# Two-layer block on one core: split-precision products with 512 activation columns, and VectorE's weight splits ahead of a tile's burst

## The chip, the core and the metric

The kernel runs on one core of a Trainium2 chip. The metric is the device time of one execution in microseconds. Three runs of the kernel before gave 3956.96, 3957.61 and 3977.92 us, median 3957.61.

## What is computed

Two transformer-like layers over 256 positions of width 2048, in float32. Their large products are with weight matrices streamed once from HBM. The change touches the output projection and the feed-forward part of each layer:

```
# layer 1
x = x + merged @ w_out                               # 2048 x 2048
up = causal_dwconv(rmsnorm(x) @ ffn_up, ffn_conv_w)  # 2048 x 11264, 3 taps
act, val = split(up, 2)
x = x + (silu(act) * val) @ ffn_down                 # 5632 x 2048
# layer 2 (no convolution; g1, g2, sh2, sc2 from a condition)
x = x + g1 * (concat(attn, rw) @ w_out_2)
h = rmsnorm(x) * (1 + sc2) + sh2
x = x + g2 * ((silu(h @ w1) * (h @ w3)) @ w2)        # widths 5632
```

## The kernel before, in words

Activations lie transposed in SBUF, 128 channels on the partitions and T = 256 positions along the free dimension. A full-precision product is made from rounded parts. ScalarE rounds a weight tile to `w_hi` and VectorE makes the remainder `w_lo = raw - w_hi`; activations have a rounded part and a remainder too (`h_hi`, `h_lo`, `f_hi`, `f_lo`, ...). For each 128x128 block of weights TensorE adds three matmuls of 256 columns in one PSUM bank: w_lo by hi, w_hi by lo, w_hi by hi (`products`, L254 to L256). Only the first 256 of a bank's 512 columns are used for that. Part of `w_in2` (L1430) already has two activations side by side, in matmuls of 512 columns.

A weight tile is 128x1024, eight such blocks. SP's queue loads tiles in pairs (1 MB) into four chunks of `raw`. `w_hi` and `w_lo` are rings of four tiles. A round is eight tiles, k = 0 to 7, one body of a hardware loop on each engine. In `ffn_up` two tiles make one result of 128 channels: the result of tiles 0 and 1 is an act part, that of tiles 2 and 3 a val part, and so on, so a round gives four results in the banks po0 to po3. There are 22 rounds in each ffn_up, 4 in each w_out, and 12 (4 loops of 24 tiles) in each ffn_down, where a result takes six tiles, the sixth of half the width.

Each engine runs its own program in order, and semaphores join them:
- ScalarE, for each k: `split_hi(k + 3)` (L235; it waits for the landed chunk and for `used`, TensorE's count of finished tiles), then the phase's body.
- VectorE, for each k: the phase's body, then `split_lo(k + 3)` (L242; it waits for `hi_ready`). LOOK = 3 is the number of tiles that the splits are ahead of TensorE.
- TensorE waits for `lo_ready` of its tile, and at a result's first tile for the bank (`free`).
- SP's queue waits for `hi_ready` and `lo_ready` before it loads over a chunk.

The bodies in ffn_up, here called bursts: in the first layer VectorE makes the convolution of an act result, three dependent operations out of the bank, into `conv_a` (k % 4 == 1, `conv`, L2635 and L2640), and frees the bank; ScalarE waits for that and makes its Silu (L1661). At k % 4 == 3 VectorE makes the convolution of the val result into `conv_v`, multiplies it with conv_a (L1686), ScalarE rounds the product to `f_hi` (L1669) and VectorE makes `f_lo` (L1695). In the second layer there is no convolution: ScalarE makes the Silu straight from the bank (L1665) and VectorE the product straight from the bank (L1691). Behind the last f_lo of the phase TensorE begins with ffn_down. In w_out and ffn_down VectorE adds each result to x out of the bank (L2698, L2391, L1721, L1718). ScalarE loads an activation table once at a round's first rounding and once at its first Silu.

Of the kernel before, what the change touches and what calls it, by code (L numbers as in the profile page):

```python
# [14 lines left out]
F32R = mybir.dt.float32r  # L15
# [6 lines left out]
P = 128  # L22
# [71 lines left out]
def program(nc, d):  # L94

    ctx = ExitStack()
    with ctx:
# [30 lines left out]
        h_hi, h_lo, hc_hi, hc_lo = hh[:, 0, 0], hh[:, 0, 1], hh[:, 1, 0], hh[:, 1, 1]  # L128
        hf = sb("hf", [KD, T], TMP)
# [62 lines left out]
        m_hi = sb("m_hi", [KD, T], A0 + 32, F32R)  # L192
        m_lo = sb("m_lo", [KD, T], A0 + 48, F32R)
        f_hi = sb("f_hi", [KF, T], A0, F32R)
        f_lo = sb("f_lo", [KF, T], A0 + 44, F32R)
# [63 lines left out]
        def project(pe, phase, rounds, act_hi, act_lo, k_tiles, r_off=0, t_off=0, split=None):  # L259
# [3 lines left out]
            with pe.Fori(0, rounds) as i:  # L263
                rnd = i + (ROUND0[phase] + r_off)
                for k in range(8):
# [3 lines left out]
                    if split is not None and k < 2:  # L269
                        pe.wait_ge(*sv.at(split, ("lo1", "lo3")[k]))  # L270
                    if half == 0:
                        turn = i * (per // 4) + (TURN0[phase] + t_off + o // 4)
                    products(pe, rnd, k, [(s, half * 8 + s) for s in range(8)], o % 4, act_hi, act_lo,
                             half == 0, half == 1 or k_tiles == 8, turn).then_inc(used, 1)

        def project_down(pe, phase):

            with pe.Fori(0, 4) as i:
                for q in range(24):
                    rnd, k, o, s = i * 3 + (ROUND0[phase] + q // 8), q % 8, q // 6, q % 6  # L280
                    tiles = [(t, s * 8 + t) for t in range(8 if s < 5 else 4)]
                    products(pe, rnd, k, tiles, o, f_hi, f_lo, s == 0, s == 5,
                             i + TURN0[phase] if s == 0 else None).then_inc(used, 1)
# [112 lines left out]
        conv_sum = sem("conv_sum")  # L396
# [960 lines left out]
        o_hi = sb("o_hi", [KD, T], H0, F32R)  # L1357
        o_lo = sb("o_lo", [KD, T], H0 + 16, F32R)
# [350 lines left out]
        def ffn_down_dve(dve, phase, f, final=False):  # L1709
            def body(i, final):  # L1710
                for q in range(24):
                    rnd = i * 3 + (ROUND0[phase] + q // 8)
                    if q % 6 == 5:
# [3 lines left out]
                        if f:  # L1717
                            dve.scalar_tensor_tensor(xt, po[o][:, 0:T], mod[:, ds(i * 4 + (80 + o), 1)], xt,  # L1718
                                                     ALU.mult, ALU.add).then_inc(free[o], 1)
                        else:  # L1720
# [1208 lines left out]
```

## Time and profile before

| | us |
|---|---|
| median of three runs | 3957.61 |
| the profiled execution | 3957.27 |
| its span, first to last instruction | 3955.6 |
| TensorE busy with matmuls | 3623.4 |
| VectorE busy | 2283.2 |
| ScalarE busy | 1655.2 |
| first ffn_up, TensorE's first to last matmul | 1067 to 1576 |
| first ffn_down | 1580 to 1836 |
| second ffn_up | 3165 to 3673 |
| second ffn_down | 3675 to 3931 |
| w_out of the layers | 953 to 1046, 3047 to 3142 |

Engines: PE is TensorE's matmul, PEld its weight load, DVE VectorE, ACT ScalarE. A row in order of time begins with its start and duration in us, and ends with the time for which the engine had been idle before it and what it waited for. A matmul's duration in such rows is longer than the distance between two of them, since they are pipelined; what counts is how often one starts. The granted clock of TensorE is 1.00 at 2.4 GHz and 0.50 at 1.2 GHz.

### The profile page before, as it was taken

How to read it: one execution, taken by the hardware profiler on the slowest of the kernel's cores; microseconds unless marked ns; L12 is line 12 of the kernel's file. 1: busy time of each engine (PE TensorE's matmuls, PEld its weight loads, DVE VectorE, ACT ScalarE, POOL GpSimd, SP SyncE). 2: the span in 40 equal slices, each digit the busy share in tenths (PEclk: the TensorE clock that was granted, in tenths of full speed). 3: DMA queues.
4: the chain of work that ended last, by engine and by line, in shares of the span. 5: the costliest groups of instructions: out<-in, count | busy, mean ns of one | idle time of the engine just before them, and what ended most of it. 6: DMA issues, size and time to landing. Idle time of an engine off the chain costs nothing.

```text
span 3955.6 us, 83548 instructions
## 1 busy us (share of the span) xinstructions
PE 3623.4 (92%) x33580; PEld 3302.6 (83%) x33580; DVE 2283.2 (58%) x4062; ACT 1655.2 (42%) x2387; POOL 24.2 (1%) x47
## 2 busy tenths in 40 slices
PE   7999998998899999997899977778788899999998
PEld 5998886878899999997688844666666899999998
DVE  4659995665577777444443533666665444444443
ACT  4545563223355554333212333443442355555333
POOL 0000000000000000000000000000000000000000
PEclk9999998999999999998899997888887999999999
DMA  4546664444355555553223363000001445555553
GB/s 156 180 145 262 257 254 165 160 171 143 134 185 176 190 180 178 176 183 133 73 96 117 139 213 117 5 7 6 7 5 57 148 170 181 182 188 178 174 181 115
DMA packets 80722, 572.11 MB, mean 145 GB/s; under 512 B 9488, under 2 KB 9744, under 8 KB 15472
## 3 DMA queue, kind: packets, MB, share of 16 engines
q1 hardware_dynamic: 78048, 558.50, 40.3%
q0 software_dynamic: 2448, 10.46, 0.8%
q8 instruction: 159, 2.61, 0.3%
q14 instruction: 67, 0.55, 0.0%
HBM read 566.82 MB, written 2.10 MB: 144 GB/s over the span
## 4 chain that ended last, share of the span: by engine, by line
PE 77%; DVE 15%; issue 3%; ACT 2%; DMA 2%; DVEq 0%; ACTq 0%; SPq 0%; POOL 0%
PE po L254 17%; PE po L255 17%; PE po L256 17%; PE po L1430 6%; DVE w_lo L242 2%; PE pa L300 2%; PE pa L989 2%; PE po L989 1%; PE po L418 1%; DMA raw<-ada 1%; DVE s_v L680 1%; PE pa L897 1%; PE po L468 1%; DVE hf L311 1%; PE po L469 1%
## 5 line engine op out<-in xcount | busy, mean ns | idle before, releaser
L242 DVE TENSOR_TENSOR w_lo<-raw,w_hi 128x1024 fp32r<-128x1024 f32 x880 | 1039.8, 1200 | 459.3 <-ACT w_hi L235 444.2
L235 ACT ACTIVATE w_hi<-raw 128x1024 fp32r<-128x1024 f32 (+1 forms) x877 | 897.8, 1037 | 803.1 <-PE po L256 582.1
L254 PE MATMUL po<-hh,w_lo 128*128 128x256 f32 x3744 | 1064.9, 284 | 24.4 <-DVE hh L335 12.6
L255 PE MATMUL po<-hh,w_hi 128*128 128x256 f32 x3744 | 1060.9, 283 | 0.0
L256 PE MATMUL po<-hh,w_hi 128*128 128x256 f32 x3744 | 1060.9, 283 | 0.0
L254 PEld LDWEIGHTS po<-hh,w_lo 128*128 128x128 f32 x3744 | 720.3, 192 | 30.4 <-issue 29.8
L255 PEld LDWEIGHTS po<-hh,w_hi 128*128 128x128 f32 x3744 | 720.3, 192 | 0.3
L256 PEld LDWEIGHTS po<-hh,w_hi 128*128 128x128 f32 x3744 | 720.1, 192 | 0.0
L254 PE MATMUL po<-f_hi,w_lo 128*128 128x256 f32 x1408 | 400.0, 284 | 6.1 <-DVE f_lo L1695 6.1
L255 PE MATMUL po<-f_lo,w_hi 128*128 128x256 f32 x1408 | 399.9, 284 | 0.0
L256 PE MATMUL po<-f_hi,w_hi 128*128 128x256 f32 x1408 | 399.8, 284 | 0.0
L254 PEld LDWEIGHTS po<-f_hi,w_lo 128*128 128x128 f32 x1408 | 271.7, 193 | 6.5 <-issue 6.5
L256 PEld LDWEIGHTS po<-f_hi,w_hi 128*128 128x128 f32 x1408 | 271.9, 193 | 0.0
L255 PEld LDWEIGHTS po<-f_lo,w_hi 128*128 128x128 f32 x1408 | 271.8, 193 | 0.0
L1430 PE MATMUL po<-hh,w_hi 128*128 128x512 f32 x704 | 218.1, 391 | 0.0
L1430 PEld LDWEIGHTS po<-hh,w_hi 128*128 128x128 f32 x704 | 133.0, 189 | 27.8
L468 PE MATMUL po<-hh,w_lo 128*128 128x256 f32 x512 | 154.3, 301 | 0.0
L1669 ACT ACTIVATE f_hi<-conv_v 128x256 f32 x88 | 36.7, 418 | 278.5 <-DVE conv_v L1686 166.1
L1430 PE MATMUL po<-hh,w_lo 128*128 128x512 f32 x352 | 137.8, 391 | 15.9 <-DVE hh L335 15.9
L470 PE MATMUL po<-hh,w_hi 128*128 128x256 f32 x512 | 145.7, 284 | 0.0
L469 PE MATMUL po<-hh,w_hi 128*128 128x256 f32 x512 | 145.5, 284 | 0.0
L300 PE MATMUL pa<-hf,ones 128*128 128x256 f32 x224 | 60.4, 437 | 53.1 <-ACT hf L291 53.1
(543 smaller groups left out, 6337.8 us busy)
## 6 DMA issues: line engine op xcount, KB each, us to landing
raw<-ffn_up SPq DMA_DIRECT2D x176, 1024.0 KB, 4.8
raw<-w_in SPq DMA_DIRECT2D x112, 1024.0 KB, 4.9
raw<-ada SPq DMA_DIRECT2D x96, 1024.0 KB, 6.3
raw<-ffn_down SPq DMA_DIRECT2D x64, 1024.0 KB, 4.9
raw<-w_out SPq DMA_DIRECT2D x32, 1024.0 KB, 4.8
raw<-ffn_down SPq DMA_DIRECT2D x32, 768.0 KB, 4.2
raw<-glu SPq DMA_DIRECT2D x16, 1024.0 KB, 6.4
raw<-dn_proj SPq DMA_DIRECT2D x8, 1024.0 KB, 5.1
```

Of the source, the lines that this page charges most:

```text
L235: act.activation(w_hi[:, k % 4, 0:width], raw[:, k // 2 % ring, (k % 2) * PW:(k % 2) * PW + width], ACT.Copy).then_inc(hi_ready, 1)
L242: dve.tensor_tensor(w_lo[:, k % 4, 0:width], raw[:, k // 2 % ring, (k % 2) * PW:(k % 2) * PW + width], w_hi[:, k % 4, 0:width].bitcast(F32 ...
L254: pe.matmul(po[bank][:, 0:T], lo, act_hi[:, t, :], start=first and n == 0, stop=False)
L255: pe.matmul(po[bank][:, 0:T], hi, act_lo[:, t, :], start=False, stop=False)
L256: mm = pe.matmul(po[bank][:, 0:T], hi, act_hi[:, t, :], start=False, stop=end)
L300: mm = pe.matmul(pa[0][:, 0:T], ones[:], hf[:, t, :], start=t == 0, stop=t == KD - 1)
L311: last = dve.scalar_tensor_tensor(out[:, t, :], x[:, t, :], w(t), rstd[:], ALU.mult, ALU.mult)
L468: pe.matmul(bank(i * per + o), lo, act_hi[:, t, :], start=first, stop=False)
L469: pe.matmul(bank(i * per + o), hi, act_lo[:, t, :], start=False, stop=False)
L470: mm = pe.matmul(bank(i * per + o), hi, act_hi[:, t, :], start=False, stop=end)
L989: mm[e] = pe.matmul(o, lhs[e][r, m, :], w, start=True, stop=True)
L1430: mm = pe.matmul(po[o % 4][:].rearrange("p (s t) -> p s t", s=2), w, hh[:, ::-1, part, t, :], start=half == 0 and n == 0 and w is lo, stop ...
```

## The change

1. `products_wide` takes the place of `products` in w_out, ffn_up and ffn_down of both layers. The rounded activations and their remainders lie side by side (`h_both`, `m_both`, `f_both`, `o_both`). For a 128x128 block there are two matmuls: w_hi by both parts, 512 columns into the whole bank, and w_lo by the rounded part, 256 columns into its first half.
2. The two halves of a bank must be added. In w_out and ffn_down `add_to_x` adds first the one and then the other to x. In ffn_up ScalarE copies the upper half to conv_a or conv_v (`upper`), VectorE adds it to the lower half in the bank (`summed`), and only then comes what came before: convolution, Silu, product.
3. `round_dve` issues `split_lo(k + LOOK)` ahead of the body in both ffn_up phases, and behind it, as before, in all others. ScalarE's order of `split_hi` and body is not changed.

The other products of the kernel (w_in, glu, dn_proj, w_in2) stay as they are. The diff, cut to its core:

```diff
+        m_both = sb("m_both", [2, KD, T], A0 + 32, F32R)
+        m_hi, m_lo = m_both[:, 0], m_both[:, 1]
+        f_both = sb("f_both", [2, KF, T], A0, F32R)
+        f_hi, f_lo = f_both[:, 0], f_both[:, 1]
...
+        def products_wide(pe, rnd, k, tiles, bank, both, first, last, turn=None):
+            if turn is not None:
+                pe.wait_ge(free[bank], turn)
+            pe.wait_ge(lo_ready, rnd * 8 + k + 1)
+            for n, (s, t) in enumerate(tiles):
+                hi = w_hi[:, k % 4, s * P:s * P + P]
+                lo = w_lo[:, k % 4, s * P:s * P + P]
+                end = last and n == len(tiles) - 1
+                pe.matmul(po[bank][:].rearrange("p (s t) -> p s t", s=2), hi, both[:, :, t, :],
+                          start=first and n == 0, stop=False)
+                mm = pe.matmul(po[bank][:, 0:T], lo, both[:, 0, t, :], start=False, stop=end)
+            return mm
...
+        def project_wide(pe, phase, rounds, both, split=None):
+            with pe.Fori(0, rounds) as i:
+                rnd = i + ROUND0[phase]
+                for k in range(8):
+                    o, half = k // 2, k % 2
+                    if split is not None and k < 2:
+                        pe.wait_ge(*sv.at(split, ("lo1", "lo3")[k]))
+                    products_wide(pe, rnd, k, [(s, half * 8 + s) for s in range(8)], o, both, half == 0, half == 1,
+                                  i + TURN0[phase] if half == 0 else None).then_inc(used, 1)
...
+        def add_to_x(dve, n, bank, xt, scale=None):
+            for h, part in enumerate(halves):
+                if h:
+                    dve.wait_ge(summed, n + 1)
+                if scale is None:
+                    last = dve.tensor_tensor(xt, po[bank][:, part], xt, ALU.add)
+                else:
+                    last = dve.scalar_tensor_tensor(xt, po[bank][:, part], scale, xt, ALU.mult, ALU.add)
+                if h == 0:
+                    last.then_inc(summed, 1)
+            return last
...
         def ffn_up_act(act, phase, f, round_act):
             def body(i, rnd, k):
                 j = i * 2 + k // 4
+                if k % 2:
+                    act.wait_ge(used, rnd * 8 + k + 1)
+                    if k % 4 == 1:
+                        act.wait_ge(ff_prod, j + KF * f)
+                    settle(act)
+                    upper_half = conv_v if k % 4 == 3 else conv_a
+                    act.activation(upper_half[:], po[k // 2][:, T:2 * T], ACT.Copy).then_inc(upper, 1)
                 if k % 4 == 1 and f == 0:
                     act.wait_ge(*freed(phase, i, 4, k // 2))
                     act.activation(conv_a[:], conv_a[:], ACT.Silu).then_inc(ff_silu, 1)
                 if k % 4 == 1 and f == 1:
-                    act.wait_ge(used, rnd * 8 + k + 1)
-                    act.wait_ge(ff_prod, j + KF)
+                    act.wait_ge(summed, i * 4 + (SUM0[phase] + k // 2 + 1))
                     act.activation(conv_a[:], po[k // 2][:, 0:T], ACT.Silu).then_inc(free[k // 2], 1)
...
                 at = i * 8 + (CONV0 + 2 * o)
+                if k % 2:
+                    n = i * 4 + (SUM0[phase] + o)
+                    dve.wait_ge(upper, i * 4 + (88 * f + o + 1))
+                    upper_half = conv_v if k % 4 == 3 else conv_a
+                    dve.tensor_tensor(po[o][:, 0:T], po[o][:, 0:T], upper_half[:], ALU.add).then_inc(summed, 1)
+                    dve.wait_ge(summed, n + 1)
                 if k % 4 == 1 and f == 0:
-                    dve.wait_ge(used, rnd * 8 + k + 1)
                     conv(dve, conv_a[:], o, w, 3, at).then_inc(free[o], 1)
                 if k % 4 == 3:
-                    dve.wait_ge(used, rnd * 8 + k + 1)
                     if f == 0:
                         conv(dve, conv_v[:], o, w, 3, at).then_inc(free[o], 1)
...
             def round_dve(dve, phase, rounds, body, r_off=0):
                 with dve.Fori(0, rounds) as i:
                     for k in range(8):
+                        if phase in ("ffn_up", "ffn_up2"):
+                            split_lo(dve, i + (ROUND0[phase] + r_off), k + LOOK)
                         body(i, i + (ROUND0[phase] + r_off), k)
-                        split_lo(dve, i + (ROUND0[phase] + r_off), k + LOOK)
+                        if phase not in ("ffn_up", "ffn_up2"):
+                            split_lo(dve, i + (ROUND0[phase] + r_off), k + LOOK)
```

`project_wide` and `project_down` call `products_wide`; the waits for SUM0 count the results of all phases.

## Rows read from the trace of the kernel before

**Rows 1.** The page: busy time, chain by line, DMA issues of ffn_up

```profile
PE 3623.4 (92%) x33580; PEld 3302.6 (83%) x33580; DVE 2283.2 (58%) x4062; ACT 1655.2 (42%) x2387; POOL 24.2 (1%) x47
...
PE po L254 17%; PE po L255 17%; PE po L256 17%; PE po L1430 6%; DVE w_lo L242 2%; PE pa L300 2%; PE pa L989 2%; PE po L989 1%; PE po L418 1%; DMA raw<-ada 1%; DVE s_v L680 1%; PE pa L897 1%; PE po L468 1%; DVE hf L311 1%; PE po L469 1%
...
raw<-ffn_up SPq DMA_DIRECT2D x176, 1024.0 KB, 4.8
```

**Rows 2.** Windows of three stages: busy us (instructions) of engines, granted clock

```profile
1067.00:1576.50 509.50, 509.29 (x4224) 509.09 (x4224) 367.32 (x524) 261.25 (x307) 0.00 (x0) 0.99 0.52 179
1580.50:1835.70 255.20, 255.16 (x2112) 254.99 (x2112) 112.20 (x111) 93.92 (x96) 0.00 (x0) 0.99 0.53 179
3165.00:3673.40 508.40, 508.35 (x4224) 508.18 (x4224) 244.54 (x269) 266.55 (x306) 0.00 (x0) 1.00 0.53 180
```

**Rows 3.** Windows: narrow products (ffn_up), wide products (w_in2)

```profile
1100.00:1550.00 450.00, 450.00 (x3752) 450.00 (x3752) 327.81 (x471) 232.18 (x274) 0.00 (x0) 1.00 0.53 182
...
1950.00:2100.00 150.00, 150.00 (x663) 124.21 (x662) 61.13 (x67) 29.16 (x28) 0.00 (x0) 1.00 0.28 97
```

**Rows 4.** ScalarE in order of time, second ffn_up: a Silu

```profile
3404.11 0.38 ACT L1665 ACTIVATE conv_a<-po 128x256 f32<-128x256 f32 x1
```

**Rows 5.** VectorE in order of time, first ffn_up: start, us, operation

```profile
1075.54 0.48 DVE L2635 TENSOR_SCALAR conv_a<-po,par 128x256 f32<-128x256 f32 x1 [5.17 <-PE po L256]
...
1190.27 1.22 DVE L242 TENSOR_TENSOR w_lo<-raw,w_hi 128x1024 fp32r<-128x1024 f32 x1 [0.62 <-ACT w_hi L235]
...
1199.64 0.42 DVE L1695 TENSOR_TENSOR f_lo<-conv_v,f_hi 128x256 f32 x1 [0.85 <-ACT f_hi L1669]
1199.98 2.35 DVE L242 TENSOR_TENSOR w_lo<-raw,w_hi 128x1024 fp32r<-128x1024 f32 x2
1202.35 0.48 DVE L2635 TENSOR_SCALAR conv_a<-po,par 128x256 f32<-128x256 f32 x1
1202.97 1.11 DVE L2640 SCALAR_TENSOR_TENSOR conv_a<-po,par,conv_a 128x255 f32<-128x255 f32 x2
1204.00 1.21 DVE L242 TENSOR_TENSOR w_lo<-raw,w_hi 128x1024 fp32r<-128x1024 f32 x1
1205.52 1.22 DVE L242 TENSOR_TENSOR w_lo<-raw,w_hi 128x1024 fp32r<-128x1024 f32 x1 [0.31 <-ACT w_hi L235]
1208.00 0.48 DVE L2635 TENSOR_SCALAR conv_v<-po,par 128x256 f32<-128x256 f32 x1 [1.26 <-PE po L256]
...
1209.87 0.43 DVE L1686 TENSOR_TENSOR conv_v<-conv_v,conv_a 128x256 f32<-128x256 f32 x1
1211.13 0.42 DVE L1695 TENSOR_TENSOR f_lo<-conv_v,f_hi 128x256 f32 x1 [0.84 <-ACT f_hi L1669]
```

**Rows 6.** Groups of w_in2 by shape: busy us, mean ns | idle before

```profile
L1458 DVE TENSOR_SCALAR zkv<-po,ts 128x512 f32 x13 | 9.8, 750 | 78.5 <-PE po L1430 78.5
```

**Rows 7.** ScalarE in order of time, first ffn_up

```profile
1199.32 1.99 ACT L235 ACTIVATE w_hi<-raw 128x1024 fp32r<-128x1024 f32 x2
1204.12 0.42 ACT L1661 ACTIVATE conv_a<-conv_a 128x256 f32<-128x256 f32 x1 [2.81 <-DVE conv_a L2640]
1204.44 1.99 ACT L235 ACTIVATE w_hi<-raw 128x1024 fp32r<-128x1024 f32 x2
...
1210.92 1.28 ACT L235 ACT_TABLE_LOAD   x1
1212.22 2.01 ACT L235 ACTIVATE w_hi<-raw 128x1024 fp32r<-128x1024 f32 x2
```

**Rows 8.** End of the first ffn_up: VectorE's last f_lo, TensorE's next matmul

```profile
1579.76 0.43 DVE L1695 TENSOR_TENSOR f_lo<-conv_v,f_hi 128x256 f32 x1 [0.84 <-ACT f_hi L1669]
...
1580.54 0.43 PE L254 MATMUL po<-f_hi,w_lo 128*128 128x256 f32 x1 [4.05 <-DVE f_lo L1695]
```

**Rows 9.** Windows of 2 us behind that gap: TensorE busy, granted clock

```profile
1582.00:1584.00 2.00, 2.00 (x12) 0.50 0.26 39
1584.00:1586.00 2.00, 2.00 (x18) 0.97 0.84 326
```

More of the change, by code:

```diff
@@ L128, in program @@
         h_hi, h_lo, hc_hi, hc_lo = hh[:, 0, 0], hh[:, 0, 1], hh[:, 1, 0], hh[:, 1, 1]
+        h_both = hh[:, 0]
         hf = sb("hf", [KD, T], TMP)
@@ L191, in program @@
         yd_lo = sb("yd_lo", [8, T], H0 + 24, F32R)
[L192 to L195, printed above, removed]
+        m_both = sb("m_both", [2, KD, T], A0 + 32, F32R)
+        m_hi, m_lo = m_both[:, 0], m_both[:, 1]
+        f_both = sb("f_both", [2, KF, T], A0, F32R)
+        f_hi, f_lo = f_both[:, 0], f_both[:, 1]
         po = [ctx.enter_context(nc.psum_tensor(f"po{n}", [P, 512], F32)) for n in range(4)]
@@ L257, in products, with project @@
             return mm
-        def project(pe, phase, rounds, act_hi, act_lo, k_tiles, r_off=0, t_off=0, split=None):
+        def products_wide(pe, rnd, k, tiles, bank, both, first, last, turn=None):
[10 more added lines that the diff above has]
+            return mm
+        def project(pe, phase, rounds, act_hi, act_lo, k_tiles, r_off=0, t_off=0):
             per = 8 if k_tiles == 8 else 4
@@ L268, in project @@
                     turn = None
-                    if split is not None and k < 2:
-                        pe.wait_ge(*sv.at(split, ("lo1", "lo3")[k]))
                     if half == 0:
@@ L281, in project_down @@
                     tiles = [(t, s * 8 + t) for t in range(8 if s < 5 else 4)]
-                    products(pe, rnd, k, tiles, o, f_hi, f_lo, s == 0, s == 5,
-                             i + TURN0[phase] if s == 0 else None).then_inc(used, 1)
+                    products_wide(pe, rnd, k, tiles, o, f_both, s == 0, s == 5,
+                                  i + TURN0[phase] if s == 0 else None).then_inc(used, 1)
+        SUM0 = {"w_out": 0, "ffn_up": 16, "ffn_down": 104, "w_out2": 120, "ffn_up2": 136, "ffn_down2": 224}
+        halves = [slice(0, T), slice(T, 2 * T)]
+        def add_to_x(dve, n, bank, xt, scale=None):
[9 more added lines that the diff above has]
+            return last
         def down_width(q):
@@ L395, in program @@
         branch_lo, ones_set = sem("branch_lo"), sem("ones_set")
-        conv_sum = sem("conv_sum")
+        conv_sum, summed, upper = sem("conv_sum"), sem("summed"), sem("upper")
         CONV0 = 72
@@ L1356, in program @@
         k_S, k_ur = pair("k_S", [P], 84.5, 0.5), pair("k_ur", [P], 85.5, 0.5)
-        o_hi = sb("o_hi", [KD, T], H0, F32R)
-        o_lo = sb("o_lo", [KD, T], H0 + 16, F32R)
+        o_both = sb("o_both", [2, KD, T], H0, F32R)
+        o_hi, o_lo = o_both[:, 0], o_both[:, 1]
         def order(e):
@@ L1716, in body @@
                         dve.wait_ge(used, rnd * 8 + q % 8 + 1)
[L1717 to L1720, printed above, removed]
-                            dve.tensor_tensor(xt, po[o][:, 0:T], xt, ALU.add).then_inc(free[o], 1)
+                        add_to_x(dve, i * 4 + (SUM0[phase] + o), o, xt,
+                                 mod[:, ds(i * 4 + (80 + o), 1)] if f else None).then_inc(free[o], 1)
                     if not final or q + LOOK < 24:
@@ L2390, in on_out @@
                     dve.wait_ge(used, rnd * 8 + k + 1)
-                    dve.scalar_tensor_tensor(xt, po[o][:, 0:T], mod[:, ds(i * 4 + (32 + o), 1)], xt,
-                                             ALU.mult, ALU.add).then_inc(free[o], 1)
+                    add_to_x(dve, i * 4 + (SUM0["w_out2"] + o), o, xt, mod[:, ds(i * 4 + (32 + o), 1)]).then_inc(free[o], 1)
             round_dve(dve, "w_out2", 4, on_out)
@@ L2425, in block2_pe @@
             rk_pe(pe)
-            project(pe, "w_out2", 4, o_hi, o_lo, 16, split=4)
+            project_wide(pe, "w_out2", 4, o_both, 4)
             norm_pe(pe, 5)
-            project(pe, "ffn_up2", 22, h_hi, h_lo, 16, split=5)
+            project_wide(pe, "ffn_up2", 22, h_both, 5)
             pe.wait_ge(ff_lo, 2 * KF)
@@ L2697, in on_out @@
                     dve.wait_ge(used, rnd * 8 + k + 1)
-                    dve.tensor_tensor(xt, po[o][:, 0:T], xt, ALU.add).then_inc(free[o], 1)
+                    add_to_x(dve, i * 4 + (SUM0["w_out"] + o), o, xt).then_inc(free[o], 1)
             round_dve(dve, "w_out", 4, on_out)
@@ L2747, in _ @@
             pe.wait_ge(mrg_lo, 16)
-            project(pe, "w_out", 4, m_hi, m_lo, 16)
+            project_wide(pe, "w_out", 4, m_both)
             norm_pe(pe, 1)
-            project(pe, "ffn_up", 22, h_hi, h_lo, 16, split=1)
+            project_wide(pe, "ffn_up", 22, h_both, 1)
             pe.wait_ge(ff_lo, KF)
```

## The prediction

> **What bounds the kernel now.** I read the page first, then the windows by stage, then TensorE's pitch, then VectorE and ScalarE in order of time within one round. The page has TensorE busy for 92% of the span and 51% of the chain of work that ended last in the three matmuls of `products`, 17% in each [rows 1]. The change touches six stages (w_out, ffn_up and ffn_down of both blocks). The windows of three of them have TensorE busy throughout, at a granted clock of 0.99 to 1.00 [rows 2]; the second ffn_down and the two w_out are like the ffn_down shown. In all six the time is the number of matmuls by their pitch. The same rows give VectorE's load: 367.3 of 509.5 us in the first ffn_up, 244.5 of 508.4 in the second, 112 of 255 in ffn_down. So there is one place where VectorE has little to spare, and it is there that I look for the next bound.
>
> **What the wider product brings.** A 256-column matmul starts every 450/3752 = 119.9 ns, a 512-column one every 150/663 = 226.2 ns, both at granted clock 1.00 [rows 3]. A weight tile costs three of the first kind today, 359.8 ns, and will cost one of each, 346.2 ns. That saves 13.7 ns a tile. No stage before has the two widths in turn, so the bounds are 0 and 13.7 ns; I take the upper one, since the wide rows already load new weights for each matmul. Tiles: 22 rounds of 64 in each ffn_up (1408, a third of the 4224 matmuls of [rows 2]), 704 in each ffn_down, 256 in each w_out. TensorE's own time then falls by 19.3 us in each ffn_up, 9.6 in each ffn_down, 3.5 in each w_out: 64.8 us in all. A round of ffn_up goes from 23.03 to 22.15 us on TensorE.
>
> The Trainium skill (TensorE: Matmul & The Clock Gate, Back-to-back issue gap) puts a warm gap at the columns over 2.4 GHz plus about 2.5 ns. By that the saving would be 2.5 ns a tile and 12 us in all. The two rows disagree with it: each has about 13 ns over its columns. The measurement decides.
>
> **What it adds.** Each result now lies in two halves of a bank. In ffn_up ScalarE copies the upper half to SBUF and VectorE adds it to the lower half in the bank, 88 times a phase, before anything else is done with it. The copy is priced by the Silu that reads the same 128x256 out of a bank, 0.38 us [rows 4]. For the add there is no VectorE arithmetic with its output in a bank. The nearest is the 128x256 product of two tensors, 0.43 us; a dependent operation starts 0.14 us behind an end (conv_a at 1202.35, 0.48 long, the next at 1202.97) [rows 5]. I take the two together, 0.57 us a step. Bounds: 0.34 us, the start-to-start of an f_lo and the w_lo behind it (1199.64 to 1199.98) [rows 5], and 0.90 us, that of the arithmetic out of a bank at 512 columns, 0.75, with the same gap [rows 6].
> In w_out and ffn_down `add_to_x` makes one operation into two, the second 0.57 us behind the first. VectorE is idle there for over half the time [rows 2], so it costs only at the phase's end: 0.6 us, four times. At the end of the second ffn_up copy and add stand before the product: 0.38 + 0.04 + 0.57 and a little for the wait, 1.1 us.
>
> **The moved split, the step that decides.** In both ffn_up phases VectorE now does `split_lo` of tile k+3 ahead of the burst of tile k. ScalarE's program keeps its order: `split_hi`, then its body, whose Silu waits for conv_a and whose f_hi waits for the product. So the split that follows a burst is now the one whose w_hi is queued behind that burst on ScalarE. Today another split lies between, with its w_hi ready long before.
> - After conv_a: today conv_a ends at 1204.08, the Silu starts at 1204.12, the next w_hi at 1204.44, and the w_lo that needs it at 1205.52 [rows 5, 7]. That is 1.44 us, of which the w_lo at 1204.00 covers all but 0.31. Moved, it stands ahead of the burst and covers nothing: VectorE waits 1.44 us, twice a round.
> - After f_lo: w_hi comes behind f_hi at 1199.32; it takes 1.04 us and 0.04 to VectorE (1204.44 to 1205.52), so its w_lo can start at 1200.40, 0.76 us after f_lo's start at 1199.64. Once a round a table load stands between: w_hi at 1212.22 gives 1213.30, 2.17 us after f_lo's 1211.13 [rows 5, 7]. Today a w_lo lies in this gap too, and the wait that is left is the 0.62 us at 1190.27 [rows 5].
>
> VectorE's chain through half a round, from the steps of [rows 5, 7]: four w_lo at 1.16, between 2.35 - 1.21 and half of 1199.98 to 1202.35 (4.64), two adds (1.14), conv_a to its end at 1204.08 (1.74 with rounding), the wait behind it (1.44), conv_v to the product (1.87), product to f_lo (1.26), f_lo to the next w_lo (0.76). That is 12.85 us; the half with the table load has 1.41 more, 14.26. A round is 27.1 us, against 22.15 on TensorE and 23.03 today. In the first ffn_up TensorE is no longer the bound. Of it 5.1 us are waits for w_hi (1.44 twice, and 0.76 and 2.17 less 0.34 each for the f_lo). Without them a round would be 22.0 us, so the adds alone use up nearly all that VectorE had spare.
>
> The Trainium skill (ScalarE: Activation LUTs, What ACT_TABLE_LOAD costs) states about 2.66 us for a switch of tables, with a drain behind the load. By it a round would be 1.4 us longer. The trace has w_hi 0.02 us behind a load of 1.28 us (1210.92 to 1212.22) [rows 7], so no drain is paid here.
>
> **The phase.** Its first conv_a starts today at 1075.54, cold clock included [rows 5]; copy and first add put the chain's start at 1076.0. From there to the last f_lo's end are 22 x 27.11 less two w_lo (2.3) and the last wait (1.7): 592.4 us, so 1668.4. Today f_lo ends at 1580.2 [rows 8]. That is +88.2 us. TensorE then sits idle for some 8 us in place of 4.05, and restarts at the lower clock for a little longer than the 3.5 us that 4.05 us of idling cost it (back to 0.97 by 1584) [rows 8, 9]: +1, an estimate.
>
> In the second ffn_up there is no conv. VectorE's chain there is 19.9 us a round (27.1 less two conv_a of 1.74 and two conv_v of 1.87), so TensorE stays the bound. The look-ahead holds too: from the end of tile 3 to w_lo of tile 7 are copy with its hand-overs 0.57, add 0.57, product 0.43 + 0.19, f_hi 0.33, table load 1.28, w_hi 1.08, w_lo 1.21 = 5.7 us, and TensorE has three tiles, 8.3 us. Weight DMAs wait in SP's queue for w_lo of a chunk freed four chunks earlier; later splits delay the issue, but their 4.8 us to landing [rows 1] fit in the five tiles, over 13 us, that remain.
>
> **The sum** against the profiled execution, 3957.27 us (span 3955.6 and 1.7 around it; the median of the runs, 3957.61, is 0.3 above it): first ffn_up +88.2 + 1.0; second -19.3 + 1.1; two ffn_down -19.2 + 1.2; two w_out -7.0 + 1.2. Together +47.2, which gives 4004 us.
>
> **The rivals.**
> - *TensorE stays the bound everywhere*, because ScalarE runs further ahead of VectorE than I have it, and look-ahead hides the waits: -64.8 and some 4.6 for longer ends give 3897. It decides if VectorE's round stays under 22.15. For it speaks only that VectorE has 28% idle time now; against it that Silu and f_hi cannot start before VectorE's burst and are ahead of the w_hi in the same queue. Chance 0.07.
> - *Half hidden*: the waits behind conv_a shrink to the 0.31 of today and the one with the table load to 0.62 [rows 5]. A round is 27.1 - 2.3 - 1.2 = 23.6 us, the first ffn_up costs 22 x 0.57 = +13 less 1 for its start, the other stages keep -41: 3928. With a round of 25.0 us the whole comes out even. Chance 0.08 for all up to 3977.
> - *The clock falls in the gaps.* TensorE will idle 5 us a round, most at once at the table load: the two w_lo before it and the one behind it span 1.16 + 7.04 us, less two tiles of 2.77, 2.7 us. After 4.05 us idle the granted clock was at its lower level for some 3.5 us [rows 8, 9]. If each round's long gap did that, TensorE would lose about 2 us of its 5 us of slack: no price. Only if it held for most of a round would TensorE be the bound, at about 33 us: 4130. Chance 0.05.
> - *The wide product saves nothing beside a narrow one*: the 45.5 us of gain in the other five stages is gone, 4050. Chance 0.05.
> - *Forecast*, VectorE's chain sets the first ffn_up at 26.4 to 28.6 us a round: 0.75.
>
> **Range.** The add's bounds move 88 steps by -0.23 and +0.33 us: -20 and +29. The new waits, each an instruction on VectorE with no row for itself, and clock losses can add to 10. 3980 to 4045 holds a little under 0.8. 0.5% of 3957 is about what a measurement of this kernel can tell from no change: faster 0.10, same 0.06, slower 0.84.
>
> **What will show it.** Right: the first ffn_up takes about 601 us to its last f_lo in place of 513, VectorE is busy for about 80% of it and its longest idle groups are w_lo waiting for ScalarE's w_hi, about 1.44 and 2.1 us each; TensorE shows gaps ahead of the matmul after a w_lo; the second ffn_up shows none and takes 489 us. Wrong: w_lo waits of 0.3 to 0.6 us in the first ffn_up with TensorE busy throughout (the rivals of hidden waits); matmul pitches that add up to 360 ns a tile (the wide product); a granted clock well under 0.9 in the first ffn_up (the clock); an add of 128x256 far from 0.43 us (its price).

## The result and the profile after

The changed kernel took 4021.25 us, the median of six runs (4001.59 to 4037.9), beside 3963.3 us for the kernel before (six runs, 3955.48 to 3984.26). The ratio on record is 1.0124, with a 95% interval of 1.0095 to 1.0152: slower by 1.2%. (The two medians divided give 1.0146, inside that interval.) Its profiled execution is the shortest of the six, 4001.59 us with a span of 3999.9, and 44.3 us of span over the one before.

The page of the changed kernel (busy time; shares of the chain that ended last, by engine and by line) answers to [rows 1]:

```profile
PE 3607.7 (90%) x28844; PEld 3062.8 (77%) x28844; DVE 2387.4 (60%) x4302; ACT 1707.8 (43%) x2563; POOL 24.2 (1%) x47
...
PE 62%; DVE 20%; issue 10%; ACT 5%; DMA 2%; DVEq 1%; ACTq 0%; SPq 0%; POOL 0%
PE po L270 19%; PE po L272 10%; PE po L1475 6%; PE po L255 3%; PE po L256 3%; PE po L257 3%; DVE w_lo L243 3%; ACT w_hi L236 2%; PE pa L345 1%; PE pa L1034 1%; PE po L1034 1%; PE po L463 1%; DMA raw<-ada 1%; DVE conv_v L2694 1%; DVE conv_a L2694 1%
```

TensorE has 28844 matmuls in place of 33580, and yet its share of the chain is down (it was 77% before), with VectorE at 20% (15%), ScalarE at 5% (2%) and issue at 10% (3%). Windows over the first ffn_up, the first ffn_down and the second ffn_up of the changed kernel (busy us and instructions of PE, PEld, DVE, ACT, POOL; granted clock; DMA) answer to [rows 2]:

```profile
1064.20:1655.60 591.40, 533.50 (x2816) 448.47 (x2816) 399.68 (x610) 281.94 (x390) 0.00 (x0) 0.96 0.44 153
1664.10:1910.50 246.40, 246.38 (x1408) 216.95 (x1408) 117.83 (x125) 93.95 (x95) 0.00 (x0) 0.99 0.55 185
3235.60:3725.40 489.80, 489.79 (x2816) 431.72 (x2816) 284.94 (x357) 295.20 (x393) 0.00 (x0) 1.00 0.53 186
```

The last two are as full of matmuls as before and shorter, 246.4 for 255.2 and 489.8 for 508.4 us. The first has a third fewer matmuls than in [rows 2], takes 591.4 us in place of 509.5, and leaves TensorE idle for 58 of them.

Span by stage in us, from TensorE's first matmul in one to its first in the next (the middle begins with the first `pa<-hf,ones` behind the first ffn_down):

| stage | before | after | difference | forecast |
|---|---|---|---|---|
| up to the first w_out | 952.6 | 950.0 | -2.6 | 0 |
| first w_out and norm | 114.6 | 114.1 | -0.5 | -2.9 |
| first ffn_up | 513.3 | 599.9 | +86.6 | +88.2 |
| first ffn_down and norm | 274.6 | 266.3 | -8.3 | -9.0 + 1.0 |
| middle, without a part of the change | 1191.9 | 1192.4 | +0.4 | 0 |
| second w_out and norm | 118.0 | 112.9 | -5.1 | -2.9 |
| second ffn_up | 510.5 | 493.0 | -17.5 | -18.2 |
| second ffn_down, norm, end | 280.1 | 271.4 | -8.7 | -9.0 |

One round of the first ffn_up, VectorE in order of time in the changed kernel (start, us, operation, idle before it); the rows answer to [rows 5]:

```profile
1180.83 0.43 DVE L1732 TENSOR_TENSOR po<-po,conv_a 128x256 f32<-128x256 f32 x1
...
1193.70 0.43 DVE L1732 TENSOR_TENSOR po<-po,conv_a 128x256 f32<-128x256 f32 x1
1194.27 0.48 DVE L2689 TENSOR_SCALAR conv_a<-po,par 128x256 f32<-128x256 f32 x1
1194.90 1.11 DVE L2694 SCALAR_TENSOR_TENSOR conv_a<-po,par,conv_a 128x255 f32<-128x255 f32 x2
1197.44 2.36 DVE L243 TENSOR_TENSOR w_lo<-raw,w_hi 128x1024 fp32r<-128x1024 f32 x2 [1.43 <-ACT w_hi L236]
1199.72 0.43 DVE L1732 TENSOR_TENSOR po<-po,conv_v 128x256 f32<-128x256 f32 x1
1200.30 0.48 DVE L2689 TENSOR_SCALAR conv_v<-po,par 128x256 f32<-128x256 f32 x1
...
1202.16 0.43 DVE L1741 TENSOR_TENSOR conv_v<-conv_v,conv_a 128x256 f32<-128x256 f32 x1
1203.45 0.42 DVE L1750 TENSOR_TENSOR f_both<-conv_v,f_both 128x256 f32 x1 [0.86 <-ACT f_both L1720]
1205.60 2.36 DVE L243 TENSOR_TENSOR w_lo<-raw,w_hi 128x1024 fp32r<-128x1024 f32 x2 [1.72 <-ACT w_hi L236]
1207.87 0.43 DVE L1732 TENSOR_TENSOR po<-po,conv_a 128x256 f32<-128x256 f32 x1
```

The two w_lo at 1197.44 and at 1205.60 stand directly behind a burst, each with an idle time for w_hi: 1.43 and 1.72 us. The add into the first bank of a half-round starts at 1180.83, 1193.70 and 1207.87: 12.87 and 14.17 us, a round of 27.04. Between their starts the rounds of this phase take 27.04 to 27.06 us, all but the first, 27.37. ScalarE in the same stretch, which answers to [rows 7]:

```profile
1196.05 0.42 ACT L1713 ACTIVATE conv_a<-conv_a 128x256 f32<-128x256 f32 x1 [3.44 <-DVE conv_a L2694]
1196.37 1.99 ACT L236 ACTIVATE w_hi<-raw 128x1024 fp32r<-128x1024 f32 x2
...
1202.78 0.42 ACT L1720 ACTIVATE f_both<-conv_v 128x256 f32 x1 [4.15 <-DVE conv_v L1741]
1203.21 1.28 ACT L236 ACT_TABLE_LOAD   x1
1204.51 2.00 ACT L236 ACTIVATE w_hi<-raw 128x1024 fp32r<-128x1024 f32 x2
```

It does the Silu at 1196.05 as conv_a ends, and only then the w_hi at 1196.37 that VectorE is waiting for; and f_hi at 1202.78, the table load, then w_hi at 1204.51. The waits of the changed kernel in that phase, 1100 to 1600 us (total, times, longest):

```profile
DVE w_lo L243 <- ACT w_hi L236: 89.9, 74, 1.7
PEld po L270 <- DVE w_lo L243: 67.5, 56, 2.7
PE po L270 <- DVE w_lo L243: 48.1, 31, 2.3
```

Here w_lo waited 89.9 us for w_hi; of that 81.5 lie in 1100 to 1550 us, the stretch in which the kernel before had 23.5. That TensorE waits for w_lo is new: the narrow kernel shows no such wait in this phase. The end of the phase, TensorE's next matmul with its idle time, against 4.05 us of idling in [rows 8]:

```profile
1664.07 0.79 PE L270 MATMUL po<-f_both,w_hi 128*128 128x512 f32 x1 [8.46 <-DVE f_both L1750]
```

### The profile page after: what moved, and what is told of

It is laid out like the page before. It is cut to its first block, busy times and chain, and to the rows that moved or that the text cites. A ratio compares the mean times of both kernels' runs of the same rounds, so it can differ in the third digit from the quotient of the medians.

```text
span 3999.9 us, 75190 instructions
## 1 busy us (share of the span) xinstructions
PE 3607.7 (90%) x28844; PEld 3062.8 (77%) x28844; DVE 2387.4 (60%) x4302; ACT 1707.8 (43%) x2563; POOL 24.2 (1%) x47
## 4 chain that ended last, share of the span: by engine, by line
PE 62%; DVE 20%; issue 10%; ACT 5%; DMA 2%; DVEq 1%; ACTq 0%; SPq 0%; POOL 0%
PE po L270 19%; PE po L272 10%; PE po L1475 6%; PE po L255 3%; PE po L256 3%; PE po L257 3%; DVE w_lo L243 3%; ACT w_hi L236 2%; PE pa L345 1%; PE pa L1034 1%; PE po L1034 1%; PE po L463 1%; DMA raw<-ada 1%; DVE conv_v L2694 1%; DVE conv_a L2694 1%
## 5 line engine op out<-in xcount | busy, mean ns | idle before, releaser
L270 PE MATMUL po<-hh,w_hi 128*128 128x512 f32 x2816 | 1015.2, 403 | 82.2 <-DVE w_lo L243 55.9
L270 PEld LDWEIGHTS po<-hh,w_hi 128*128 128x128 f32 x2816 | 539.7, 192 | 225.5 <-DVE w_lo L243 78.0
L270 PE MATMUL po<-f_both,w_hi 128*128 128x512 f32 x1408 | 490.4, 394 | 11.6 <-DVE f_both L1750 11.6
L272 PE MATMUL po<-f_both,w_lo 128*128 128x256 f32 x1408 | 393.2, 279 | 0.0
L270 PEld LDWEIGHTS po<-f_both,w_hi 128*128 128x128 f32 x1408 | 264.8, 188 | 72.0 <-issue 12.2
L272 PEld LDWEIGHTS po<-f_both,w_lo 128*128 128x128 f32 x1408 | 266.5, 189 | 0.0
L256 PE MATMUL po<-hh,w_hi 128*128 128x256 f32 x928 | 262.7, 283 | 0.0
L257 PE MATMUL po<-hh,w_hi 128*128 128x256 f32 x928 | 262.7, 283 | 0.0
L1475 PE MATMUL po<-hh,w_hi 128*128 128x512 f32 x704 | 217.8, 391 | 0.0
L256 PEld LDWEIGHTS po<-hh,w_hi 128*128 128x128 f32 x928 | 178.1, 192 | 0.3
L257 PEld LDWEIGHTS po<-hh,w_hi 128*128 128x128 f32 x928 | 178.1, 192 | 0.0
L1475 PEld LDWEIGHTS po<-hh,w_hi 128*128 128x128 f32 x704 | 133.1, 189 | 27.6
L515 PE MATMUL po<-hh,w_hi 128*128 128x256 f32 x512 | 145.8, 285 | 0.0
L514 PE MATMUL po<-hh,w_hi 128*128 128x256 f32 x512 | 145.5, 284 | 0.0
```

The costliest lines, as they stand in the source:

```text
L256: pe.matmul(po[bank][:, 0:T], hi, act_lo[:, t, :], start=False, stop=False)
L257: mm = pe.matmul(po[bank][:, 0:T], hi, act_hi[:, t, :], start=False, stop=end)
L270: pe.matmul(po[bank][:].rearrange("p (s t) -> p s t", s=2), hi, both[:, :, t, :], start=first and n == 0, stop=False)
L272: mm = pe.matmul(po[bank][:, 0:T], lo, both[:, 0, t, :], start=False, stop=end)
L514: pe.matmul(bank(i * per + o), hi, act_lo[:, t, :], start=False, stop=False)
L515: mm = pe.matmul(bank(i * per + o), hi, act_hi[:, t, :], start=False, stop=end)
```

## The experiments

Theory: the w_lo behind a burst waits for a w_hi which ScalarE's queue holds behind the same burst; with the adds in the burst, VectorE's chain is longer than TensorE's round. Rivals: the copies and adds alone are more than VectorE can do; or the clock, which falls in TensorE's gaps, sets the time of a round. Phase lengths below are of the first ffn_up, first matmul to ffn_down's first, 513.3 us before and 599.9 after.

**1. The split back behind the burst**, in the changed kernel:

```diff
-                        if phase in ("ffn_up", "ffn_up2"):
-                            split_lo(dve, i + (ROUND0[phase] + r_off), k + LOOK)
                         body(i, i + (ROUND0[phase] + r_off), k)
-                        if phase not in ("ffn_up", "ffn_up2"):
-                            split_lo(dve, i + (ROUND0[phase] + r_off), k + LOOK)
+                        split_lo(dve, i + (ROUND0[phase] + r_off), k + LOOK)
```

> The changed kernel with one part undone: VectorE's burst comes ahead of split_lo again in both ffn_up phases; wide products, copies and adds stay. Theory (the split behind a burst waits for a w_hi that is queued behind that burst on ScalarE): the waits of w_lo for w_hi in the first ffn_up fall from 1.43 and 1.72 us to 0.3 to 0.6, a round takes 23.4 us in place of 27.0, the phase loses about 79 us, and the whole is 3922 us against 4001.6 of the changed kernel's profiled execution, under the 3957 of before. Rival (the copies and adds are what VectorE cannot carry, whatever the order): a round stays within 1 us of 27.0 and the whole at about 4000. Rival (the clock falls in TensorE's gaps and sets the pace): the gaps stay, since the adds stay, and the whole is over 3970.

The phase took 531.0 us, 68.9 less than in the changed kernel. The whole was 3955.35 us at a ratio of 0.9972 (0.9954 to 0.9989) to the kernel before. Two adds of VectorE one round apart, and the total wait of w_lo (1100 to 1550 us):

```profile
1305.55 0.43 DVE L1732 TENSOR_TENSOR po<-po,conv_a 128x256 f32<-128x256 f32 x1
...
1329.44 0.43 DVE L1732 TENSOR_TENSOR po<-po,conv_a 128x256 f32<-128x256 f32 x1
...
DVE w_lo L243 <- ACT w_hi L236: 22.7, 57, 0.6
```

The rounds here take 23.9 us, 0.5 over the forecast, and the wait of w_lo for w_hi is 22.7 us for the changed kernel's 81.5, with the copies and adds still there. The rival of the adds expected 27 us and is out; that of the clock expected a whole over 3970. Yet with the better order the wide phase is still 17.7 us longer than the narrow one. In the second ffn_up the order makes no difference: 493.0 us here and in the changed kernel. The profiled execution, 3961.5 us, is 39 over the forecast: 10 in this phase, 17 in the middle, where the change has no part and this execution took 1209.6 us, 7 ahead of the first w_out and 5 in the last ffn_down. Number 8 deals with the middle and with ffn_down. The 7 us stay unexplained: that first stretch, the same in all kernels, took 950.0 to 957.8 us over the profiles.

**2. The order alone**, in the kernel before, which keeps its narrow products and has no adds:

```diff
                     for k in range(8):
+                        if phase in ("ffn_up", "ffn_up2"):
+                            split_lo(dve, i + (ROUND0[phase] + r_off), k + LOOK)
                         body(i, i + (ROUND0[phase] + r_off), k)
-                        split_lo(dve, i + (ROUND0[phase] + r_off), k + LOOK)
+                        if phase not in ("ffn_up", "ffn_up2"):
+                            split_lo(dve, i + (ROUND0[phase] + r_off), k + LOOK)
```

> The kernel before with one part added: split_lo ahead of the burst in both ffn_up phases; products stay at 256 columns, no copies, no adds. Theory: without the adds VectorE's chain through a round is 27.1 less 4 x 0.57, that is 24.8 us, over TensorE's 23.03, so the first ffn_up takes about 36 us longer and the whole is 3993 us; the second ffn_up is unchanged. Rival (the order alone is free, and only wide products with it cost time): 3957 us, rounds of 23.03.

3995.16 us, ratio 1.0083 (1.0050 to 1.0115); the phase took 547.9 us, 34.6 more than before. Two f_lo of VectorE one round apart, 24.65 us, and the wait of w_lo, now four times the 23.5 us of before:

```profile
1312.49 0.42 DVE L1695 TENSOR_TENSOR f_lo<-conv_v,f_hi 128x256 f32 x1 [0.85 <-ACT f_hi L1669]
...
1337.14 0.42 DVE L1695 TENSOR_TENSOR f_lo<-conv_v,f_hi 128x256 f32 x1 [0.85 <-ACT f_hi L1669]
...
DVE w_lo L242 <- ACT w_hi L235: 90.7, 73, 1.8
```

The order costs 35 us without the adds and 69 with them (number 1): half of its price is there with the narrow burst already. The other half is most simply read as slack that the adds have used up, since the narrow round had been set by TensorE; no run shows it by itself.

**3. ScalarE's w_hi ahead of its part of the burst**, in the changed kernel:

```diff
                     act.activation(upper_half[:], po[k // 2][:, T:2 * T], ACT.Copy).then_inc(upper, 1)
+                    if k < 7 or not last_round:
+                        split_hi(act, rnd, k + 1 + LOOK)
...
-            round_act(act, phase, 22, body)
+            split_hi(act, ROUND0[phase], LOOK)
+            def ahead(i, last_round=False):
+                for k in range(8):
+                    if k % 2:
+                        split_hi(act, i + ROUND0[phase], k + LOOK)
+                    body(i, i + ROUND0[phase], k, last_round)
+            with act.Fori(0, 21) as i:
+                ahead(i)
+            ahead(21, True)
```

> The changed kernel, with ScalarE's order changed as well: in ffn_up it issues the w_hi of tile k+4 right behind the copy of tile k's upper half and ahead of the Silu or f_hi, so the w_lo behind a burst finds its w_hi ready. Theory: the waits of 1.43 us go, a round is VectorE's busy time and inner waits, 22.0 to 23.1 us against TensorE's 22.15; the first ffn_up takes about 85 us less than in the changed kernel, the whole is 3916 us. Rival (VectorE is loaded beyond its share whoever makes w_hi ready): over 3960.

3941.86 us, ratio 0.9939 (0.9916 to 0.9961). The phase took 519.1 us, 81 less than in the changed kernel, with VectorE's order as the change has it. Two adds one round apart (23.33 us) and the wait of w_lo:

```profile
1418.97 0.43 DVE L1742 TENSOR_TENSOR po<-po,conv_a 128x256 f32<-128x256 f32 x1
...
1442.30 0.43 DVE L1742 TENSOR_TENSOR po<-po,conv_a 128x256 f32<-128x256 f32 x1
...
DVE w_lo L243 <- ACT w_hi L236: 21.2, 58, 0.5
```

VectorE does the same work in the same order, and 81 of the 87 us are gone, because another engine's queue was changed. That is the theory's main test. The round of 23.33 us is a little over the 22.0 to 23.1 expected; w_lo still waits 21.2 us for w_hi in 450 us, about 1.1 us a round. The expectation had the wait gone. The whole is 26 us over its forecast: 4 in this phase, 10 in the second ffn_up (503.5 us, a slower pace of matmuls), 8 ahead of the first w_out and 2 in the second.

**4. Half of the table loads**, in the changed kernel:

```diff
-            round_act(act, phase, 22, body)
+            with act.Fori(0, 11) as i2:
+                for h in range(2):
+                    i = i2 * 2 + h
+                    for k in range(8):
+                        split_hi(act, i + ROUND0[phase], k + LOOK)
+                        body(i, i + ROUND0[phase], k)
```

> The changed kernel with ScalarE's ffn_up loops over two rounds in one body, so that the two table loads come once in two rounds; nothing else. Theory: every second wait of 1.72 us at the first w_lo behind an f_lo falls to 0.31; rounds alternate between 27.0 and 25.7 us, the first ffn_up takes 14 us less, the whole is 3987 us. Rival (the load is hidden behind something else that is late): 4000 to 4003.

The phase took 584.4 us, 15.5 less for 11 loads fewer ahead of a w_hi, 1.4 us each: the 1.28 us of the load stood wholly on the chain. The rounds alternate between 27.05 and 25.64 us, as forecast. The whole, 4007.52 us at 1.0119 (1.0084 to 1.0154), doesn't tell this apart from the changed kernel. In the profile half of the saving was lost again ahead of the first w_out (957.8 us for 950.0) and 3.9 us in the first ffn_down, at a slower pace of matmuls.

**5. The narrow kernel with the early split and ScalarE ahead**, number 2 with ScalarE's loop as in number 3:

```diff
             def body(i, rnd, k, last_round=False):
                 j = i * 2 + k // 4
+                if k % 2:
+                    act.wait_ge(used, rnd * 8 + k + 1)
+                    if k < 7 or not last_round:
+                        split_hi(act, rnd, k + 1 + LOOK)
...
```

> The narrow kernel with split_lo first, as in the run before of that kind (548 us in the first ffn_up, 3995 us), and ScalarE's w_hi of tile k+4 ahead of its Silu and f_hi. Theory (the order costs time only since w_hi is queued behind the burst): the waits of w_lo for w_hi go, TensorE is the bound again with rounds of 23.03 us, the first ffn_up takes 513 us and the whole is that of the kernel before, 3957 us, within 5. Rival (VectorE's early split costs time by itself): over 3975.

3964.93 us, ratio 1.0001 (0.9982 to 1.0021), phase 513.8 us for the 513.3 of before. Number 2's 34.6 us are gone but for 0.5. The profiled execution took 3979.7 us; 19 us of that lie in the middle. ScalarE now waits for TensorE, w_lo waits for w_hi less than half as long as in number 2 (34.9 us for 90.7), and TensorE waits for neither (1100 to 1550 us):

```profile
ACT w_hi L235 <- PE po L256: 125.4, 97, 1.9
...
DVE w_lo L242 <- ACT w_hi L235: 34.9, 59, 1.0
```

**6. A third of the matmul time left out.** In the first ffn_up the matmul with w_lo is not made, so the remainder of the weights is missing from its results:

```diff
-                pe.matmul(po[bank][:].rearrange("p (s t) -> p s t", s=2), hi, both[:, :, t, :],
-                          start=first and n == 0, stop=False)
+                mm = pe.matmul(po[bank][:].rearrange("p (s t) -> p s t", s=2), hi, both[:, :, t, :],
+                               start=first and n == 0, stop=skip and end)
+                if skip:
+                    continue
...
```

> The changed kernel with a part of the computation left out: in the first ffn_up TensorE makes only the matmul of 512 columns for each block, the one with w_lo is not made, so TensorE's work in a round falls from 22.15 to 14.5 us at full clock. Everything of VectorE and ScalarE stays. Theory (VectorE's chain with its waits for ScalarE sets the phase): rounds of 27.0 us, the first ffn_up takes 600 us as before, at most 6 us more if the clock stays at its lower level, where 64 matmuls of 512 columns take 27.3 us. Rival (TensorE, by its gaps and its clock, has a share in the 27.0 us): the phase falls by over 20 us.

This kernel ran once, in 4027.97 us. The phase took 597.6 us against 599.9. Matmuls were half as many, TensorE was busy for 352.6 of 500 us, the granted clock fell to 0.84 (0.96 in the changed kernel), and TensorE's longest wait in a round grew from 2.3 to 4.2 us. The window, and the matmuls behind one such gap (those behind the next start at 1211.09, a round of 27.03 us):

```profile
1100.00:1600.00 500.00, 352.59 (x1184) 264.81 (x1184) 338.17 (x517) 240.87 (x335) 0.00 (x0) 0.84 0.44 155
...
1184.06 10.37 PE L270 MATMUL po<-hh,w_hi 128*128 128x512 f32 x32 [4.21 <-DVE w_lo L243]
```

With a third less to do on TensorE, and a lower clock, the round is the same: neither has a share in the 27.0 us. That ends the rival of the clock.

**7. The whole change out of the first ffn_up only**; the other five stages stay wide:

```diff
-            project_wide(pe, "ffn_up", 22, h_both, 1)
+            project(pe, "ffn_up", 22, h_hi, h_lo, 16, split=1)
...
-                if k % 2:
+                if k % 2 and f == 1:
                     act.wait_ge(used, rnd * 8 + k + 1)
...
-                        if phase in ("ffn_up", "ffn_up2"):
+                        if phase == "ffn_up2":
...
```

> The changed kernel with the whole change taken out of the first ffn_up alone (three matmuls of 256 columns, no copies, no adds, burst first); the other five stages stay wide. Theory: the first ffn_up is back at 513 us, the others keep what they gained in the changed kernel's profile (8.3 + 17.5 + 8.7 + 0.5 + 5.1 = 40 us), so the whole is 3917 us where matmul pairs start every 346 ns, and up to 22 us more (3328 pairs of 6.6 ns) where they start every 353 ns, as they did in single stages of the last two profiles. Rival (the wide product saves nothing that lasts): 3957.

3933.63 us, ratio 0.9915 (0.9892 to 0.9938). The phase is at 513.2 us. This version beats both kernels, by 0.85% and about 2%. It is near the upper end of the 3917 to 3939 us expected. In its profile (3938.97 us) both ffn_down stages ran at the slower pace that number 8 looks into, 10 us together, and the middle was 10 us longer than in the changed kernel's.

**8. What the two paces come from.** A pair is the two matmuls of one 128x128 block, 512 columns and 256. In the profiles of numbers 3 and 4 some wide stages took 353 ns for a pair in place of 346; so did the first w_out of the changed kernel's own profile. Two kernels put a tile's eight matmuls of 512 columns ahead of its eight of 256, one on number 7 and one on the changed kernel; a third is the changed kernel again:

```diff
                 pe.matmul(po[bank][:].rearrange("p (s t) -> p s t", s=2), hi, both[:, :, t, :],
                           start=first and n == 0, stop=False)
+            for n, (s, t) in enumerate(tiles):
+                lo = w_lo[:, k % 4, s * P:s * P + P]
+                end = last and n == len(tiles) - 1
                 mm = pe.matmul(po[bank][:, 0:T], lo, both[:, 0, t, :], start=False, stop=end)
```

> The kernel of the run before it in this set, with a weight tile's eight matmuls of 512 columns first and its eight of 256 behind them, in place of one of each in turn. Theory of the two paces (346 or 353 ns a pair comes from the widths in turn; wide ones in a row took 226.2 and narrow ones 119.9 in all profiles): every stage shows 346 ns, the whole is 3917 us with a narrower spread. Rival (the pace belongs to the execution or the stage, not to the order): some stages show 353 ns again and the spread is that of the run before.

> The changed kernel with its products grouped in the same way, eight of 512 columns and then eight of 256; nothing else. Theory: in the first ffn_up VectorE's chain sets the time, rounds of 27.0 us as in the changed kernel whatever TensorE's order; in the other stages 346 ns a pair in every one; the whole is 4000 us with a spread of under 15 us. Rival (TensorE's pace matters in the first ffn_up too): its rounds differ from 27.0.

> The changed kernel once more, unchanged, for a second profile beside the first, whose 3999.9 us of span was the shortest of six. Theory: rounds of 27.0 us in the first ffn_up again; what is longer lies in the other stages, as pairs of matmuls at 353 ns in place of 346 (up to 22 us in all), and in the recurrences of the second layer (its middle, which took 1192 to 1210 us in the profiles so far, with no part of the change in it). Rival (the first ffn_up varies, by the clock in TensorE's gaps): its rounds differ from 27.0 by over 0.3 us.

The second ffn_up in windows of 350 us (busy us and matmuls of PE first), the changed kernel's first profile:

```profile
3250.00:3600.00 350.00, 350.00 (x2021) 308.74 (x2021) 202.78 (x252) 213.92 (x285) 0.00 (x0) 1.00 0.54 188
```

The changed kernel again, its first ffn_up and its second:

```profile
1065.70:1657.30 591.60, 533.80 (x2816) 448.89 (x2816) 399.64 (x610) 282.13 (x390) 0.00 (x0) 0.96 0.44 153
3300.00:3650.00 350.00, 350.00 (x1984) 303.36 (x1983) 198.47 (x248) 210.96 (x280) 0.00 (x0) 1.00 0.53 185
```

Grouped, on number 7:

```profile
3200.00:3550.00 350.00, 350.00 (x2009) 308.11 (x2008) 201.10 (x250) 211.88 (x282) 0.00 (x0) 1.00 0.53 187
```

These are 2 x 350 / 2021 = 346.4 ns a pair, 352.8, and 348.4; taken from start to start, 346.6, 353.3 and 349.1. Nothing differs between the first two programs. In a stage in which TensorE does not stop, the pace held from its first microseconds to its last, and it changed from stage to stage. Grouping gave a time in between (349.1 ns from start to start in every wide stage of both grouped kernels but the first ffn_up, where TensorE waits), not the 346 that the theory of the order wanted, so that theory fell. The wholes were 3934.09 us at 0.9921 (0.9891 to 0.9951), 4015.81 us at 1.0143 (1.0111 to 1.0175) and 4027.04 us at 1.0145 (1.0116 to 1.0174): no gain from grouping that can be told. What sets the pace stays open, but the traces show when it is set. In number 3's first ffn_up TensorE stops for a moment about every 12 us, and each run of matmuls between two stops has one of the two paces: 30 pairs from 1138.34 to 1148.74 us, 346.8 ns each, and 30 from 1161.66 to 1172.26, 353.3 ns each. A stop can change the pace, and between stops it stays.

The first ffn_up took 599.8 us grouped and 600.2 us in the repetition, against 599.9: it does not vary. The 35 us between the two profiles of the changed kernel lie in the middle (1209.5 us for 1192.4, 17), in the second ffn_up (502.3 for 493.0, 9) and in the ffn_down behind it (278.7 for 271.4, 7), both at 353 ns. The middle contains the second layer's recurrence, where TensorE has short matmuls with gaps between. From its first matmul `pa<-k_S,k_ah` to its last (TensorE's busy time, granted clock), in the changed kernel and in its repetition:

```profile
2559.10:3104.30 545.20, 439.61 (x9086) 0.85 0.02 6
...
2556.50:3123.10 566.60, 464.39 (x9087) 0.79 0.02 6
```

The same matmuls take 25 us more of TensorE's time at the lower clock, and the stretch is 21 us longer; the rest of the middle is 4 us shorter. Over all twelve profiles the stretch's length goes with the clock, from 540.6 us at 0.87 (the kernel before) to 565.3 at 0.78 (number 1). This speaks for the clock as the source of the difference, though no run sets it, and why it is lower there in one execution than in another isn't shown.

## Why the prediction was right

Forecast 4004 us, measured 4001.6 in the profile with 4021 as the median, on the side and within the range.

- **The bound moves to VectorE in the first ffn_up.** Right, to the term. Chain: 27.11 us a round forecast, 27.04 measured. Waits behind conv_a: 1.44 forecast, 1.43. With the table load, from f_lo's start to w_lo's: 2.17 forecast, 2.15 measured (1203.45 to 1205.60). Add: 0.57 a step forecast, 0.57 from 1193.70 to 1194.27; its 0.43 us with the output in a bank are those of the product with the output in SBUF. Numbers 3, 5 and 6 show that it is ScalarE's queue and not TensorE or the order by itself.
- **The phase.** +88.2 forecast, +86.6 measured. TensorE's gap at its end was 8.46 us for the 8 forecast.
- **The other five stages.** -42.0 us forecast, and +1.0 for the restart that falls into the first ffn_down; -40.1 measured. That this sum fits so well is in part luck. The two w_out, forecast at -2.9 each, came at -0.5 and -5.1: the first ran at the slower pace, and of the second's gain up to 2.3 us may be none, since that stage took 115.7 us in the narrow kernel of number 5 and 118.0 in that of before. The second ffn_up has no wait of TensorE for w_lo, as the look-ahead of 5.7 against 8.3 us said.
- **The wide product.** The forecast's 13.7 ns is for a 128x128 block, which it calls a tile; from start to start it is 360.0 less 346.6, 13.4 ns. That held in all but one of the five stages of this profile that are bound by TensorE, and it is the best case: at 353 ns a pair the saving is 7 ns. Over the 3328 blocks of these stages the slower pace costs up to 21 us. It was not among the rivals.
- **The median.** The 17 us between forecast and median were not foreseen, and that the profiled execution, the shortest of six, came within 3 us of the forecast is luck to that extent. The forecast started from 3957 us, and the kernel before has a median of 3963.3 over six runs: 6 of the 17 us. The first profile, like the forecast, has the good pace nearly everywhere and a short middle. The repetition has 17 us more in the middle and 16 in two stages at the slow pace. The middle took 1185 to 1211 us over the eleven profiles of the changed kernel and the experiments, 1191.9 in that of before; its length goes with the granted clock in the recurrence (number 8), in narrow and wide kernels alike.
- **The rival of hidden waits** named the right point, a round under TensorE's. Number 3 is that case, made by moving w_hi, and its round is 23.3 us; number 1 is at 23.9. Neither gets under 22.15, so even then the wide products don't pay in this phase: 519 and 531 us against 513. A wide kernel with both orders mended, burst first and w_hi ahead, was not run.
- **What to see in the profile.** VectorE was to be busy for about 80% of the phase and was for 399.7 of 591.4 us, 68%. That figure counted the gaps between dependent operations as work; they are on the chain but are not busy time. The wait with the table load was put at 2.1 us there and is 1.72 of idling: the 2.15 less f_lo's own 0.42.
- **The clock.** The rival's first half came true, and cost nothing, as it said. Behind TensorE's long gap, which ends at 1206.88 us in this round, the granted clock is at its lower level for a few microseconds (TensorE's busy time, granted clock):

```profile
1208.00:1210.00 2.00, 2.00 (x8) 0.50 0.94 291
1210.00:1212.00 2.00, 2.00 (x10) 0.69 0.55 234
1212.00:1214.00 2.00, 2.00 (x13) 1.00 0.00 0
```

  This happens in 14 of the 22 rounds, which makes the 0.96 of the phase, and the rounds with it are as long as those without. Number 6 shows the same at 0.84.

The Trainium skill (TensorE: Matmul & The Clock Gate, Back-to-back issue gap) gives about 2.5 ns over the columns at 2.4 GHz, and gives it for an isolated matmul; for a stream with a weight load for each matmul it has about 131 ns at 512 columns. The pairs here have 26.4 ns over their 768 columns at 2.4 GHz (320 ns) for two matmuls, or 33, and 512 columns took 226.2 ns [rows 3], so neither number of the page holds here. The saving in the better pace is the 13 or so ns that one matmul less brings, as the rows had it.

## What to carry to other kernels

When two engines share a pipeline, moving an instruction ahead on one of them changes which of the other's results it needs first. Look in the other's queue for what stands before that result: here a `w_lo` that was moved ahead of a burst left the next one waiting for a `w_hi` that ScalarE makes behind the same burst. Before a matmul is made cheaper at another engine's cost, sum that engine's whole dependent chain for one round, waits included, against the new TensorE round; where it is longer, keep the old form in that stage alone, which here turned a loss of 1.2% into a gain of 0.85%.

## What was not expected of the hardware

A 512-column matmul and one of 256 in turn start every 346.6 or every 353.3 ns, in the same program at a granted clock of 1.00. The pace holds until TensorE stops, for a whole stage where it doesn't, and can be the other one behind the stop. In the better pace the distances from start to start are about 230 and 117 ns in turn; in the other they repeat after three pairs (232, 118, 241, 120, 235, 114 ns in the repetition's second ffn_up). Of 256 columns only, a matmul starts every 120 ns wherever TensorE doesn't wait, in each profile, and of 512 only, every 226 to 227 ns. The middle, between the first ffn_down and the second w_out and the same code in all kernels, took from 1185 to 1211 us, with the granted clock in its recurrence between 0.87 and 0.78.
